# Transposing instructions in place of products with the identity, and a passage between two blocks without a phase barrier

## The chip, the cores and the metric

The kernel runs on one core of a Trainium2 chip. The metric is the device time of one execution in microseconds. A core has five engines with instruction streams of their own: PE (TensorE, matrix products into eight PSUM banks), DVE (VectorE), ACT (ScalarE), POOL (GpSimd) and SP (SyncE, which here issues the weight transfers). They meet through semaphores only.

## What is computed

Two blocks run one after the other on 256 tokens of width 1024, all in float32. The first: a token mixer, then 16 experts that each choose 34 of 272 tokens, then a norm. The second: a mixer with two branches (a gated delta rule and RWKV-7), whose context part does not depend on the first block, then a mixture of 32 experts in four groups. Cut to what the change touches:

```python
# end of block 1
y = einsum(hid, w_down) * g[..., None]           # 16 experts, scattered and added to h
h = h + y
x = _rmsnorm(h, final_norm_g)                    # over all 1024 columns, times a row of gains
# start of block 2
u = modulate(rmsnorm(x, norm_mix_g_2), shift, scale)
cols = u @ w_in_2                                # the mixer's projections
```

So two norms follow each other: the final norm of block 1 gives `x`, and the norm ahead of mixer 2 needs the sum of squares of `x`, that is of the normed rows times the gains.

## The kernel before

The kernel is one hand-written program; each engine's stream is written out in its own function, and the order in the code is the order on the engine. SP's queue carries almost all transfers, in order of issue. Weights pass through a ring of 6 slots: piece `n` may be issued once piece `n-6` has been used (`issue`, semaphore `piece_used`).

**Experts of block 1.** For each expert PE multiplies the gathered tokens `xsT` with eight gate and eight up pieces (`gate_up_pe`, L3026), turns the hidden rows with transposing instructions (`turn_hid_pe`, L3036) and multiplies with eight down pieces (`down_pe`, L3049). The context part of block 2 is threaded through this stage as a coroutine on each engine (`context_pe`, `context_dve`, `context_act`); there its helper `heads` (L2749) makes 128x128 products, some of them with the identity matrix `ident`, which turn a tile.

**The passage.** At the end the last pair of experts is added to the rows (`combine_pe`, L3056, into four banks; `add_rows_dve`, L1730, four adds). Then all engines meet at a barrier (`phase_ended`). SP loads the row of gains `g_rows` (L870) behind this barrier. ACT squares and sums each of the two row tiles and takes the roots (`norm_act`, L280 and L283), DVE takes reciprocals and scales (`norm_dve`, L290 and L292), DVE multiplies with the gains (L566), and the same norm runs once more for mixer 2: ACT L280 and L283, DVE L290 and L292 into `cn`. PE turns `cn` with 16 transposing instructions (`transposed_norm_pe`, L274) into eight banks, DVE applies modulation, one bank after the other, into `u2x_lat` (L2046), and after a second barrier PE starts the first projection of mixer 2 (`by_feature`, L303, two groups of 32 products each).

**Later.** In the gated delta rule beta is spread over rows by products with the identity (L3176), each between three other products of its head (L3174, L3177, L3178); DVE waits for these sixteen products of a direction (L2125). `row_of_columns_pe` (L3430) turns 32 columns, each spread over 128, by 32 products of 128x128 with the identity; ACT copies each eight of them out as a row (`row_act`, L1412) and takes a root in between (L1418), which waits for DVE's sum (L2342). In the mixture of experts each pair of experts runs: 32 products with gate and up (L3506), gathers (L3488), four products with the 64x64 identity that turn the hidden rows (L3515), gathers, eight products with down (L3529). Ten slots hold the weights there; SP issues a piece when its slot has been used.

`nc.tensor.transpose` and a product with the identity give the same tile: data as the loaded operand, identity streamed. The first is the engine's transposing form. In the trace a float32 product leaves two records, as L303 does with 64 products and 128 records, and a transposing instruction leaves one (L274: 16 and 16).

## Time and profile before

| | us |
|---|---|
| median of 3 runs | 2850.74 (2850.65 to 2860.58) |
| profiled execution | 2856.64 |
| its span | 2854.8 |
| PE busy | 2476.3 (87%) |
| DVE busy | 926.6 (32%) |
| ACT busy | 449.8 (16%) |

The span runs from the first to the last instruction of the profiled execution, and 1.84 us of its time lie outside. A busy share is an average over stages with different limits; the rows further below are of single stages. In a row, L3026 is line 3026 of the kernel before; `128*34 128x462` is a product with a loaded operand of 128 rows and 34 columns and a streamed one of 128 rows and 462 columns.

### The profile page before, as it was taken

The page shows a single profiled execution, that of the slowest core. Times are in us where ns is not written, and L with a number is a line of the kernel's source. Part 1 is how long each engine was busy: PE and PEld are TensorE (multiplying, and loading weights), DVE is VectorE, ACT ScalarE, POOL GpSimd, SP SyncE. Part 2 cuts the span into 40 slices and gives each one's busy share as a digit, 9 for nine tenths or more (in the row PEclk, how much of TensorE's full clock was granted, in tenths as well). Part 3 has the DMA queues.
Part 4 walks back from the last instruction along what each step waited for, and adds up shares of the span by engine and source line. Part 5 has one row for each costly group of instructions (what it writes and reads, how often), then busy time and mean ns, then how long its engine had stood idle before and what let it go on. Part 6 is the DMA issues. An engine that isn't in the chain of part 4 may idle for free. (4 is left out here: it accounts for less than half of the span.)

```text
span 2854.8 us, 43435 instructions
## 1 busy us (share of the span) xinstructions
PE 2476.3 (87%) x19563; PEld 1351.4 (47%) x19563; DVE 926.6 (32%) x1788; ACT 449.8 (16%) x810; POOL 85.1 (3%) x93
## 2 busy tenths in 40 slices
PE   6978588988999988999999999877686889689995
PEld 4524234333343333534444444355665888355553
DVE  1216733410423212241313141147547440332222
ACT  1022100110101010121211221022023220000001
POOL 0001000000000000000000000000000100000000
PEclk9987787999999999999999999978888999799998
DMA  5314433799999998999999999941010024359996
GB/s 183 118 59 157 168 138 152 316 411 393 419 406 415 417 417 370 380 417 416 411 416 406 415 398 418 413 157 60 2 38 1 3 94 148 144 235 422 422 422 282
DMA packets 129425, 789.13 MB, mean 276 GB/s; under 512 B 17473, under 2 KB 19785, under 8 KB 65113
## 3 DMA queue, kind: packets, MB, share of 16 engines
q1 hardware_dynamic: 125785, 773.78, 67.3%
q0 software_dynamic: 3456, 12.58, 1.1%
q8 instruction: 154, 2.52, 0.4%
q14 instruction: 30, 0.25, 0.0%
HBM read 774.79 MB, written 11.53 MB: 275 GB/s over the span
## 5 line engine op out<-in xcount | busy, mean ns | idle before, releaser
L3026 PE MATMUL bank<-ring,arena 128*34 128x462 f32 (+1 forms) x3072 | 673.5, 574 | 76.9 <-DMA ring<-in_w_up 58.2
L3026 PEld LDWEIGHTS bank<-ring,arena 128*34 128x34 f32 x3072 | 179.8, 113 | 434.9 <-issue 408.2
L3049 PE MATMUL bank<-ring,arena 128*34 128x512 f32 (+1 forms) x1536 | 340.2, 559 | 1.1 <-DVE arena L2032 0.6
L3049 PEld LDWEIGHTS bank<-ring,arena 128*34 128x34 f32 x1536 | 105.3, 112 | 217.0 <-issue 193.7
L303 PE MATMUL bank<-arena,ring 128*128 128x256 f32 (+1 forms) x688 | 161.1, 397 | 3.9 <-DVEq L2049 1.8
L303 PEld LDWEIGHTS bank<-arena,ring 128*128 128x128 f32 x688 | 135.7, 198 | 30.5 <-DVEq L2049 2.2
L2025 DVE TENSOR_TENSOR arena<-arena,bank 34x462 f32<-34x462 f32 (+1 forms) x96 | 95.3, 1081 | 154.1 <-ACT arena L1097 153.8
L1097 ACT ACTIVATE arena<-bank 34x462 f32<-34x462 f32 (+1 forms) x96 | 85.8, 1038 | 195.9 <-PE bank L3026 195.8
L3506 PE MATMUL bank<-ring,arena 128*64 128x256 f32 x992 | 111.1, 379 | 3.0 <-DMA ring<-in_moe_w_up 2.2
L313 PE MATMUL bank<-ring,arena 128*128 128x512 f32 (+1 forms) x224 | 98.8, 596 | 0.0
L2924 PEld LDWEIGHTS bank<-arena 64*64 64x64 f32 x2304 | 72.8, 134 | 48.3 <-issue 47.8
L3506 PEld LDWEIGHTS bank<-ring,arena 128*64 128x64 f32 x992 | 72.8, 137 | 45.1 <-issue 12.3
L3488 PE MATMUL bank<-arena 128*128 128x512 f32 (+1 forms) x160 | 82.6, 648 | 5.8 <-DVE arena L2505 5.8
L3422 PE MATMUL bank<-arena,ring 128*128 128x256 f32 x384 | 83.1, 379 | 0.0
L2924 PE MATMUL bank<-arena 64*64 64x64 f32 x2304 | 82.7, 221 | 0.0
L1981 DVE TENSOR_TENSOR arena<-arena,bank 128x256 f32<-128x256 f32 x40 | 15.0, 418 | 200.5 <-PE bank L2924 200.5
L3422 PEld LDWEIGHTS bank<-arena,ring 128*128 128x128 f32 x384 | 72.9, 190 | 9.9
L1132 ACT ACTIVATE arena<-bank 128x512 f32<-128x512 f32 x42 | 25.1, 597 | 318.8 <-PE bank L2924 212.7
L3529 PE MATMUL bank<-ring,arena 128*64 128x512 f32 x264 | 65.2, 624 | 2.7 <-issue 2.0
L2737 PE MATMUL bank<-arena,ring 128*128 128x256 f32 x288 | 64.2, 381 | 2.8 <-DMA ring<-in_w_in 2.8
L353 PE MATMUL bank<-ring,arena 128*128 128x512 f32 (+1 forms) x136 | 63.5, 622 | 3.6 <-DVE arena L2367 2.7
L954 POOL TENSOR_TENSOR arena<-arena 128x256 f32<-128x256 f32 (+1 forms) x16 | 26.6, 1662 | 1285.1 <-ACT arena L1221 1284.4
(634 smaller groups left out, 2904.1 us busy)
## 6 DMA issues: line engine op xcount, KB each, us to landing
ring<-in_w_gate SPq DMA_DIRECT2D x128, 1408.0 KB, 12.8
ring<-in_w_up SPq DMA_DIRECT2D x128, 1408.0 KB, 12.5
ring<-in_w_down SPq DMA_DIRECT2D x128, 1408.0 KB, 10.9
ring<-in_w_in SPq DMA_DIRECT2D x46, 1024.0 KB, 6.9
ring<-in_moe_w_down SPq DMA_DIRECT2D x33, 1024.0 KB, 15.3
ring<-in_moe_w_gate SPq DMA_DIRECT2D x31, 1024.0 KB, 13.3
ring<-in_moe_w_up SPq DMA_DIRECT2D x31, 1024.0 KB, 16.1
ring<-in_ada_w SPq DMA_DIRECT2D x24, 1024.0 KB, 7.0
```

The source lines that it names most:

```text
L303: last = mm(ps[base + ct][:, 0:n_toks], w[:, k, ct * P:(ct + 1) * P], x[:, half * kts + k, :], start=half + k == 0, stop=half == len(views ...
L313: last = mm(ps[base + t][:r, 0:w.shape[2]], x[:, half * kts + k, off:off + r], w[:, k, :], start=half + k == 0, stop=half == len(views) - ...
L1097: ACTV(hid_rows(c), in_rows(ps[c][0:CAP, 0:n]), ACT.Silu).then_inc(silu_done, up(silu_done))
L2025: TT(hid_rows(c), hid_rows(c), in_rows(ps[c][SLOT:SLOT + CAP, 0:n]), ALU.mult).then_inc(hid_done, up(hid_done))
L2737: last = mm(bank_a[:, ct % 2 * SEQ:(ct % 2 + 1) * SEQ], views[k // 4][0][:, k % 4, ct * P:(ct + 1) * P], u2x_ctx[:, k, :], start=k == 0, s ...
L2924: last = mm(dst[r, q, :], lhs[r, q, :], rhs[r, q, :], start=True, stop=True)
L3026: last = mm(ps[c][row:row + CAP, 0:n], xsT[:, e, k, :], w[:, at:at + n], start=k == 0, stop=k == KT - 1)
L3049: last = mm(ps[6][row:row + CAP, c:c + n], hidT[:, j, :], w[:, at - m * PIECE:at - m * PIECE + n], start=j == 0, stop=j == FT - 1)
L3422: last = mm(ps[base + ct // 2][:, ct % 2 * SEQ:(ct % 2 + 1) * SEQ], views[k // kts][0][:, k % kts, ct * P:(ct + 1) * P], x[:, k, :], start ...
L3488: last = mm(ps[gather_bank(g, k)][:, 0:group_cols(g)], xn2_by8[:, t, k, :], oh[g % 2][:, t, 0:group_cols(g)], start=t == 0, stop=t == 1)
L3506: last = mm(ps[4][CAP2 * which:CAP2 * (which + 1), m * DE:(m + 1) * DE], x, weights[which][:, k, :], start=k == 0, stop=k == KT - 1)
L3529: last = mm(ps[6 + half][CAP2 * m:CAP2 * (m + 1), :], hidT2[:, f, CAP2 * m:CAP2 * (m + 1)], w[:, f, half * BANK:(half + 1) * BANK], start= ...
```

## The change

Two things change. Products with the identity become transposing instructions: 48 in the context part (keys, values, beta of the delta rule, values of RWKV), 16 for beta (L3176), 32 in `row_of_columns_pe` and 78 in the mixture of experts. Other products with the identity stay.

The passage is rewritten. The first barrier is gone; PE, ACT and DVE go on by semaphores. DVE multiplies the un-normed rows with the gains at once (`scaled`), ACT sums the squares of the rows and of `scaled`, and the factor of the second norm is worked out from both sums on columns, so that one scaling with two factors gives `cn`. The rows `x1` themselves are scaled at the end, behind the modulation. PE turns `cn` tile by tile, and the first products of mixer 2 wait for four of the eight parts of `u2x_lat` (`ready`), not for a barrier. ACT asks for a root early, on a column that nobody reads, so that the table of roots is loaded then. SP loads `g_rows` ahead of the first piece of the seventh expert, and the first six pieces of mixer 2 right behind the last piece of the experts.

```diff
-        def by_feature(pe, base, views, x, n_toks):
+        def by_feature(pe, base, views, x, n_toks, ready=None):
             for half, (w, slot, count, _) in enumerate(views):
                 pe.wait_ge(slot, count)
+                if ready:
+                    pe.wait_ge(ready, due(pe, ready, w.shape[1]))
...
+        squares = xsT_flat[:, 2 * D:4 * D].rearrange("p (t d) -> p t d", t=2)
+        scaled = u2[:, 0:2, :]
+        scaled_sum, scaled_std, rstd_sq = st4[:, 0:2], st4[:, 2:4], den2[:, 0:2]
...
@@ SP
-            issue(tables_at, n_experts)
-            sp.wait_ge(phase_ended, N_PHASES_1 * 4)
+            gain_at = gate_up_pieces[6][0][0][3]
+            issue(tables_at, gain_at)
+            sp.wait_ge(piece_used, after(gate_up_pieces[3][KT - 1]))
             sp.dma_start(g_rows, A["final_norm_g"].partition_broadcast(P)).then_inc(g_rows_landed, up(g_rows_landed, 16))
+            issue(gain_at, n_experts)
+            issue(n_gdn - 8, n_gdn - 2)
             sp.wait_ge(final_ready, due(sp, final_ready))
             sp.dma_start(flat7, consts[2]).then_inc(join7_landed, up(join7_landed, 16))
-            issue(n_gdn - 8, n_gdn - 2)
@@ ACT
-            act.drain().then_inc(phase_ended, 1)
-            act.wait_ge(phase_ended, phase_end(act))
-            final_norm_act(act, x1)
-            act.wait_ge(final_ready, due(act, final_ready))
-            norm_act(act, x1, TILES2, cn)
+            ACTV(ss[:, 2:3], eps_col, ACT.Sqrt)
+            for t in range(2):
+                act.wait_ge(x_ready, due(act, x_ready))
+                ACTV(squares[:, t, :], x1[:, t, :], ACT.Square, accum_out=ss[:, t:t + 1]).then_inc(act_order, up(act_order))
+            act.wait_ge(act_order, own(act, act_order))
+            ACTV(ss[:, 0:2], ss[:, 0:2], ACT.Sqrt, scale=1.0 / D, bias=eps_col).then_inc(norm_std_ready, up(norm_std_ready))
+            for t in range(2):
+                act.wait_ge(x_ready, due(act, x_ready))
+                ACTV(squares[:, t, :], scaled[:, t, :], ACT.Square, accum_out=scaled_sum[:, t:t + 1]).then_inc(act_order, up(act_order))
+            act.wait_ge(act_order, own(act, act_order))
+            act.wait_ge(sqrt_asked, due(act, sqrt_asked))
+            for t in range(2):
+                ACTV(scaled_std[:, t:t + 1], scaled_sum[:, t:t + 1], ACT.Sqrt,
+                     scale=rstd_sq[:, t:t + 1], bias=eps_col).then_inc(norm_std_ready, up(norm_std_ready))
@@ DVE
-                signal = x_ready if (t, half) == HALVES[-1] else dve_order
+                signal = x_ready if half else dve_order
                 add_rows_dve(t, half, 2 * t + half, signal)
             dve.wait_ge(x_ready, own(dve, x_ready))
-            dve.drain().then_inc(phase_ended, 1)
-            dve.wait_ge(phase_ended, phase_end(dve))
             dve.wait_ge(g_rows_landed, due(dve, g_rows_landed, 16))
-            final_norm_dve(dve, x1, x1)
+            for t in range(2):
+                TT(scaled[:, t, :], x1[:, t, :], g_rows, ALU.mult).then_inc(x_ready, up(x_ready))
-            norm_dve(dve, x1, TILES2, cn)
+            dve.wait_ge(norm_std_ready, due(dve, norm_std_ready))
+            nc.vector.reciprocal(rstd[:, 0:2], ss[:, 0:2]).then_inc(dve_order, up(dve_order))
+            dve.wait_ge(dve_order, own(dve, dve_order))
+            STT(rstd_sq, rstd[:, 0:2], 1.0 / D, rstd[:, 0:2], ALU.mult, ALU.mult).then_inc(sqrt_asked, up(sqrt_asked))
+            dve.wait_ge(x_ready, own(dve, x_ready))
+            for t in range(2):
+                dve.wait_ge(norm_std_ready, due(dve, norm_std_ready))
+                nc.vector.reciprocal(scaled_std[:, t:t + 1], scaled_std[:, t:t + 1]).then_inc(dve_order, up(dve_order))
+                dve.wait_ge(dve_order, own(dve, dve_order))
+                TS(cn[:, t, :], scaled[:, t, :], rstd[:, t:t + 1], scaled_std[:, t:t + 1], ALU.mult, ALU.mult).then_inc(xn_ready, up(xn_ready))
             for k in range(KT):
                 dve.wait_ge(xnT_ready, due(dve, xnT_ready))
                 TS(u2x_lat[:, k, :], ps[k][:, 0:SEQ], gains[:, k, 0:1], mods[:, k, 0:1],
                      ALU.mult, ALU.add).then_inc(u2x_ready, up(u2x_ready))
-                dve.wait_ge(u2x_ready, own(dve, u2x_ready))
+            for t in range(2):
+                last = TS(x1[:, t, :], scaled[:, t, :], rstd[:, t:t + 1], None, ALU.mult)
+            last.then_inc(final_ready, up(final_ready))
@@ PE
+            for t in range(2):
+                pe.wait_ge(xn_ready, due(pe, xn_ready))
+                for k in range(KT):
+                    last = nc.tensor.transpose(ps[k][:, t * P:(t + 1) * P], cn[:, t, k * P:(k + 1) * P], ident)
+                    if t == 1:
+                        last.then_inc(xnT_ready, up(xnT_ready))
             pe.drain().then_inc(phase_ended, 1)
-            pe.wait_ge(phase_ended, phase_end(pe))
-            pe.wait_ge(xn_ready, due(pe, xn_ready))
-            transposed_norm_pe(pe, TILES2, cn)
-            pe.drain().then_inc(phase_ended, 1)
-            pe.wait_ge(phase_ended, phase_end(pe))
+            phase_end(pe)
-            by_feature(pe, 0, gdn_pieces[0], u2x_lat, SEQ)
+            by_feature(pe, 0, gdn_pieces[0], u2x_lat, SEQ, u2x_ready)
@@ row_of_columns_pe (L3430); in the same way the other places
-                    last = mm(ps[base + k // 4][:, k % 4 * P:(k % 4 + 1) * P], column(k).to_broadcast([P, P]), ident,
-                              start=True, stop=True)
+                    last = nc.tensor.transpose(ps[base + k // 4][:, k % 4 * P:(k % 4 + 1) * P], column(k).to_broadcast([P, P]), ident)
```

On DVE the passage reads as follows before, from the last adds to the modulation; what a row waits for stands in brackets, and several instructions of one kind in a row are counted (x2).

```order
L1730 TENSOR_TENSOR arena<-arena,bank 128x512 [waits banks_filled] x4
L290 RECIPROCAL small<-small 128x1 [waits x_ready,norm_std_ready,g_rows_landed,phase_ended]
L292 TENSOR_SCALAR arena<-arena,small 128x1024 [waits dve_order]
L290 RECIPROCAL small<-small 128x1 [waits norm_std_ready,dve_order]
L292 TENSOR_SCALAR arena<-arena,small 128x1024 [waits dve_order]
L566 TENSOR_TENSOR arena<-arena 128x1024 [waits xn_ready]
L566 TENSOR_TENSOR arena<-arena 128x1024 [waits dve_order]
L290 RECIPROCAL small<-small 128x1 [waits norm_std_ready,final_ready]
L292 TENSOR_SCALAR arena<-arena,small 128x1024 [waits dve_order]
L290 RECIPROCAL small<-small 128x1 [waits norm_std_ready,dve_order]
L292 TENSOR_SCALAR arena<-arena,small 128x1024 [waits dve_order]
L2046 TENSOR_SCALAR arena<-bank,arena 128x256 [waits xnT_ready,xn_ready]
```

After the change the same stretch of DVE's stream is this.

```order
L1736 TENSOR_TENSOR arena<-arena,bank 128x512 [waits banks_filled] x4
L2046 TENSOR_TENSOR arena<-arena 128x1024 [waits g_rows_landed,x_ready]
L2046 TENSOR_TENSOR arena<-arena 128x1024
L2049 RECIPROCAL small<-small 128x2 [waits norm_std_ready]
L2051 SCALAR_TENSOR_TENSOR small<-small 128x2 [waits dve_order]
L2055 RECIPROCAL small<-small 128x1 [waits norm_std_ready,x_ready]
L2057 TENSOR_SCALAR arena<-arena,small 128x1024 [waits dve_order]
L2055 RECIPROCAL small<-small 128x1 [waits norm_std_ready]
L2057 TENSOR_SCALAR arena<-arena,small 128x1024 [waits dve_order]
L2060 TENSOR_SCALAR arena<-bank,arena 128x256 [waits xnT_ready] x8
L2063 TENSOR_SCALAR arena<-arena,small 128x1024 x2
```

The multiplication with the gains (1024 columns, two of them) moved ahead of both norms, one long scaling per tile is left between the sums and the modulation, and the scaling of `x1` (the last row) moved behind the modulation.

On PE the passage before runs from the last adds into banks to the first products of mixer 2.

```order
L3056 MATMUL bank<-arena 128x512 [waits y_read,banks_read]
L3056 MATMUL bank<-arena 128x512 x3
L274 MATMUL bank<-consts,arena 128x128 [waits xn_ready,phase_ended]
L274 MATMUL bank<-consts,arena 128x128 x15
L303 MATMUL bank<-arena,ring 128x256 [waits slot0_landed,phase_ended]
L303 MATMUL bank<-arena,ring 128x256 x15
L303 MATMUL bank<-arena,ring 128x256 [waits slot1_landed]
```

After the change PE's stream is this.

```order
L3078 MATMUL bank<-arena 128x512 [waits y_read,banks_read]
L3078 MATMUL bank<-arena 128x512 x3
L3137 MATMUL bank<-consts,arena 128x128 [waits xn_ready]
L3137 MATMUL bank<-consts,arena 128x128 x7
L3137 MATMUL bank<-consts,arena 128x128 [waits xn_ready]
L3137 MATMUL bank<-consts,arena 128x128 x7
L305 MATMUL bank<-arena,ring 128x256 [waits u2x_ready,slot0_landed]
L305 MATMUL bank<-arena,ring 128x256 x15
L305 MATMUL bank<-arena,ring 128x256 [waits u2x_ready,slot1_landed]
```

The waits for `phase_ended` are gone, the turning waits once for each tile, and the products wait for `u2x_ready` in two halves.

SP's queue before, from the last pieces of the experts to the constants of the mixer (`in_final_norm_g` is the row of gains, `const` a table for the delta rule):

```order
L852 DMA ring<-in_w_up 128x2816 [waits piece_used]
L852 DMA ring<-in_w_down 128x2816 [waits piece_used] x9
L870 DMA arena<-in_final_norm_g 128x1024 [waits phase_ended]
L872 DMA arena<-const 128x1088 [waits final_ready]
L852 DMA ring<-in_w_in 128x4x512 [waits piece_used] x6
L878 DMA arena<-in_gdn_a_log 128x8 [waits phase_ended]
```

After the change, first the place of the gains in the middle of the experts, then the end of the experts:

```order
L849 DMA ring<-in_w_up 128x2816 [waits piece_used]
L849 DMA ring<-in_w_down 128x2816 [waits piece_used]
L868 DMA arena<-in_final_norm_g 128x1024 [waits piece_used]
L849 DMA ring<-in_w_gate 128x2816 [waits piece_used]
L849 DMA ring<-in_w_up 128x2816 [waits piece_used]
...
L849 DMA ring<-in_w_down 128x2816 [waits piece_used] x9
L849 DMA ring<-in_w_in 128x4x512 [waits piece_used] x6
L872 DMA arena<-const 128x1088 [waits final_ready]
L877 DMA arena<-in_gdn_a_log 128x8 [waits phase_ended]
```

The gains moved from behind the experts to a place among the pieces of the seventh expert, and the six pieces of `in_w_in` moved ahead of the wait for `final_ready`.

## Rows read from the trace of the kernel before

**Rows 1.** Busy time of the engines by stretch; at the end clock, DMA share, GB/s.

```profile
1180.00:1850.00 670.00, 638.25 (x5749) 277.33 (x5750) 170.23 (x327) 126.42 (x255) 26.60 (x16) 0.99 1.00 413
...
1878.00:1893.00 15.00, 9.21 (x29) 7.76 (x30) 6.44 (x16) 2.01 (x6) 0.00 (x0) 0.50 1.03 373
1894.00:1918.00 24.00, 24.00 (x113) 21.12 (x112) 10.04 (x22) 3.55 (x6) 0.00 (x0) 1.00 0.52 161
2336.00:2344.00 8.00, 7.75 (x66) 7.57 (x67) 7.34 (x8) 5.16 (x10) 0.00 (x0) 1.00 0.90 333
2478.00:2490.00 12.00, 10.66 (x48) 10.18 (x48) 3.81 (x11) 0.00 (x0) 0.00 (x0) 0.50 1.01 427
...
2600.00:2742.00 142.00, 142.00 (x876) 81.87 (x874) 38.33 (x62) 10.69 (x18) 4.80 (x9) 1.00 1.01 422
```

**Rows 2.** Timeline of PE between the blocks: start, us; in brackets the idle time before.

```profile
1864.04 3.67 PE L3056 MATMUL bank<-arena 128*128 128x512 f32 x8 [1.38 <-ACT arena L1106]
1881.97 3.65 PE L274 MATMUL bank<-consts,arena 128*128 128x128 f32 x16 [14.26 <-DVE arena L292]
1887.44 30.95 PE L303 MATMUL bank<-arena,ring 128*128 128x256 f32 x128 [1.82 <-DVEq L2049]
```

**Rows 3.** Timeline of DVE between the blocks.

```profile
1867.74 0.69 DVE L1730 TENSOR_TENSOR arena<-arena,bank 128x512 f32<-128x512 f32 x1 [0.17 <-PE bank L3056]
...
1873.76 0.75 DVE L292 TENSOR_SCALAR arena<-arena,small 128x1024 f32<-128x1024 f32 x1
1874.55 2.48 DVE L566 TENSOR_TENSOR arena<-arena 128x1024 f32<-128x1024 f32 x2
1879.88 0.16 DVE L290 RECIPROCAL small<-small 128x1 f32<-128x1 f32 x1 [2.85 <-ACT small L283]
...
1882.74 4.60 DVE L2046 TENSOR_SCALAR arena<-bank,arena 128x256 f32<-128x256 f32 x8 [0.92 <-PE bank L274]
```

**Rows 4.** Timeline of ACT between the blocks.

```profile
1868.51 1.06 ACT L280 ACTIVATE arena<-arena 128x1024 f32<-128x1024 f32 x1 [4.62 <-DVEq L2038]
...
1870.86 1.28 ACT L283 ACT_TABLE_LOAD   x1
1872.15 0.62 ACT L283 ACTIVATE small<-small 128x1 f32<-128x1 f32 x2
```

**Rows 5.** Timeline of the DMA issues of SP between the blocks.

```profile
1877.43 8.09 SPq L852 DMA_DIRECT2D ring<-in_w_in  x6
```

**Rows 6.** DMA issues, 1860 to 1876 us: KB, us from issue to landing.

```profile
arena<-in_final_norm_g SPq DMA_DIRECT2D x1, 512.0 KB, 3.8
```

**Rows 7.** Line 3149, transposing: records, length in ns (least, median, most), first and last start.

```profile
L3149 PE MATMUL bank<-consts,arena x16: 272/273/307, 1956.1 to 1958.6; 128*128 128x128 f32 x16
```

**Rows 8.** Timeline of PE: eight transposing instructions of line 3149.

```profile
1956.13 1.04 PE L3149 MATMUL bank<-consts,arena 128*128 128x128 f32 x8
```

**Rows 9.** Timeline of PE: eleven transposing instructions of 34 rows.

```profile
1838.84 0.87 PE L3036 MATMUL bank<-consts,arena 34*128 34x34 f32 x11
```

**Rows 10.** Line 3430, products with the identity: records, lengths in ns, first and last start.

```profile
L3430 PE MATMUL bank<-consts,arena x64: 275/275/347, 2336.1 to 2343.2; 128*128 128x128 f32 x64
```

**Rows 11.** Timeline of DVE where it waits for the products around line 3176.

```profile
1970.96 0.69 DVE L2125 TENSOR_TENSOR arena<-bank,arena 128x512 f32<-128x512 f32 x1 [5.66 <-PE bank L3178]
...
1974.51 0.69 DVE L2125 TENSOR_TENSOR arena<-bank,arena 128x512 f32<-128x512 f32 x1 [2.39 <-PE bank L3178]
```

**Rows 12.** Timeline of DVE beside `row_of_columns_pe`.

```profile
2339.80 1.22 DVE L2342 TENSOR_REDUCE arena<-arena 128x16 f32<-128x1024 f32 x1
```

**Rows 13.** Timeline of ACT beside `row_of_columns_pe`.

```profile
2341.00 1.28 ACT L1418 ACT_TABLE_LOAD   x1
```

**Rows 14.** Chain that ended last, mixture of experts: start, us, what.

```profile
2595.95 1.08 PE bank L3515 x8
...
2798.47 22.89 DMA ring<-in_moe_w_up
...
2826.10 0.70 PE bank L3515 x4
```

More of the change, by code:

```diff
@@ L557, in filled_with_pair @@
             return KT + PAIRS + 2 * (2 * i + EARLY + 1)
-        def final_norm_act(act, src):
-            norm_act(act, src, TILES2, u2)
-        def final_norm_dve(dve, src, dst):
-            norm_dve(dve, src, TILES2, u2)
-            for t in range(2):
-                signal = final_ready if t else dve_order
-                TT(dst[:, t, :], u2[:, t, :], g_rows, ALU.mult).then_inc(signal, up(signal))
-                dve.wait_ge(signal, own(dve, signal))
-        g_rows = xsT.rearrange("p e k s -> p (e k s)")[:, 0:D]
+        xsT_flat = xsT.rearrange("p e k s -> p (e k s)")
+        g_rows = xsT_flat[:, 0:D]
+        squares = xsT_flat[:, 2 * D:4 * D].rearrange("p (t d) -> p t d", t=2)
+        scaled = u2[:, 0:2, :]
+        scaled_sum, scaled_std, rstd_sq = st4[:, 0:2], st4[:, 2:4], den2[:, 0:2]
         final_ready, g_rows_landed = sem("final_ready"), sem("g_rows_landed")
         x1 = h1[:, 1:3, :]
-        N_PHASES_1 = 7
+        N_PHASES_1 = 6
         phases_before_second = N_PHASES_1
@@ L956, in _ @@
                         pool.wait_ge(steps7_ready, own(pool, steps7_ready))
-            pool.drain().then_inc(phase_ended, 1)
-            pool.wait_ge(phase_ended, phase_end(pool))
             pool.drain().then_inc(phase_ended, 1)
@@ L2744, in project, with turned_heads @@
                             copied_by_act(token)
+                def turned_heads(dst, src):
+                    for h in range(4):
+                        last = nc.tensor.transpose(dst[:, h * P:(h + 1) * P], src(h), ident)
+                    return last
                 def heads(dst, lhs, rhs):
@@ L2788, in context_pe @@
                     pe.wait_ge(turned_read, due(pe, turned_read))
-                    heads(bank_a, lambda h: kT_c[:, h, c * P:(c + 1) * P], lambda h: ident).then_inc(turned, up(turned))
+                    turned_heads(bank_a, lambda h: kT_c[:, h, c * P:(c + 1) * P]).then_inc(turned, up(turned))
                 yield from until(slot_number(1, 2))
@@ L2906, in context_pe @@
                     for q in range(4):
-                        last = mm(bank_a[0:C7, q * P:(q + 1) * P], vT7c[:, q, c * C7:(c + 1) * C7], ident, start=True, stop=True)
+                        last = nc.tensor.transpose(bank_a[0:C7, q * P:(q + 1) * P], vT7c[:, q, c * C7:(c + 1) * C7], ident)
                     token = for_dve(last)
@@ L3175, in _ @@
                            start=True, stop=True)
-                        mm(ps[b0 + 1][:, hs], beta[:, c, e:e + 1].to_broadcast([P, P]), ident, start=True, stop=True)
+                        nc.tensor.transpose(ps[b0 + 1][:, hs], beta[:, c, e:e + 1].to_broadcast([P, P]), ident)
                         last = mm(ps[b0 + 2][:, hs], kT[:, h, toks], kT[:, h, toks], start=True, stop=True)
@@ L3514, in _ @@
                     for m, tau in enumerate(tiles_of(i)):
-                        last = mm(ps[4][:, f * P + m * CAP2:f * P + (m + 1) * CAP2], hid2_by2[0:CAP2, m, f, :],
-                                  ident[0:CAP2, 0:CAP2], start=True, stop=True)
+                        last = nc.tensor.transpose(ps[4][:, f * P + m * CAP2:f * P + (m + 1) * CAP2], hid2_by2[0:CAP2, m, f, :],
+                                                   ident[0:CAP2, 0:CAP2])
                 last.then_inc(hidT_ready, up(hidT_ready))
```

4 lines of the change are left out of this document (2 added, 2 removed).

## The prediction

> **What bounds the kernel now.** I read the stages first, by the busy time of the engines in stretches, because the 87% of PE are an average. In the second half of the experts of block 1 the transfers run at a DMA share of 1.00 and 413 GB/s while PE is busy 638 of 670 us; in the mixture of experts, 2600 to 2742 us, the DMA share is 1.01 at 422 GB/s and PE is busy all of the 142 us [rows 1]. In both stages PE and the transfers are close to each other, and the reader should see that taking work from PE there need not bring time. Between these stages the DMA is mostly free and a chain of PE, DVE and ACT sets the time.
>
> The passage is such a chain. The timelines show PE finish its last adds, stand idle 14.26 us, turn 16 tiles, and idle 1.82 us more before the projection [rows 2]. From DVE's last add (1867.74 + 0.69 = 1868.43) to the first product of L303 (1887.44) pass 19.0 us [rows 2, 3]. Transfers aren't late in it: the row of gains takes 3.8 us [rows 6] beside ACT's first norm, and the products at 1887.44 were released by DVE [rows 2].
>
> **The passage after the change.** I lay out the new chain with the durations of before, allowing some 0.1 us for each handover.
> - ACT sums a tile in (1870.86 − 1868.51)/2 = 1.18 us and takes a root in 0.31; the table load of 1.28 moves into ACT's idle time ahead of the last add [rows 4]. The first tile's sum fits ahead of the last add too. The second tile: 1868.5 to 1869.7, both roots in one instruction to 1870.0.
> - Beside it DVE multiplies with the gains, 2.48 us [rows 3], to 1871.0, and then makes two small columns of some 0.16 each [rows 3] by 1871.4. This multiplication was on the chain; now it is beside ACT's sum for its first half.
> - ACT sums the scaled tiles from 1870.0 to 1872.4; the first root is there at 1872.7.
> - DVE: reciprocal 0.16 and scaling 0.75 [rows 3], first tile at 1873.75, second at 1874.75. The scaling has two factors now. No row has that over 1024 columns in SBUF; below it costs 0.75, above 1.3 us (the multiplication's 1.24 rounded up). I take 0.75, since it is the same instruction and size as L292.
> - PE turns the first tile from 1873.9. L274 took 3.65 us for 16 at the granted clock 0.50 (1.2 GHz) [rows 1, 2], and an instruction has 0.42 of drain, so 0.215 each: the first bank is complete at 1873.9 + 8 × 0.215 + 0.42 = 1876.0.
> - DVE modulates in 4.60/8 = 0.575 us a bank [rows 3]; four banks, 1878.4. PE may start at 1878.5.
>
> So PE starts 1887.4 − 1878.5 = **8.9 us** earlier; 8.0 if the scalings cost their upper bound, 9.8 if PE turns at 2.4 GHz, where one costs 0.11 (below). What was put behind costs nothing: scaling `x1` (two of 0.75) ends near 1882.3, and ACT and DVE are next wanted when PE has finished 32 products of the first group, which alone took about half of 30.95 us [rows 2]. SP's six pieces of `in_w_in`, issued from 1877.43 before [rows 5], go out as slots come free and land while PE idles. Every stage behind follows this chain, and later transfers are issued off it, so the gain should reach the end.
>
> **The gains' transfer** moves into the saturated experts. 512 KB at 413 GB/s are **1.3 us** of a queue that ends the stage [rows 1, 6]. Bounds: nothing, if PE is the later one just there; 3.8 us, its whole time from issue to landing when alone [rows 6].
>
> **Transposing instructions.** The identity products leave two records each: L3430 has 64 for 32 products, first start to last (2343.2 − 2336.1)/63 = 0.113 us a record [rows 10], so 0.225 a product. Eight transposing ones take 1.04 us with a last one of 0.27 [rows 7, 8], so (1.04 − 0.27)/7 = 0.11 each. A turned 128x128 tile thus saves 0.115 us. The Trainium skill's page "TensorE: Matmul & The Clock Gate", section "Terms", calls the transposing mode four times faster for float32. The rows say twice, and they decide; by the page a product would save 0.17 and the beta term below would be 2.7 instead of 1.8.
> - Beta (L3176), 16 products: DVE waits 5.66 and 2.39 us for exactly these groups [rows 11], so 16 × 0.115 = **1.8 us** are on the chain. Bounds 0.9 (one direction hidden) and 3.6 (all at 1.2 GHz, at twice the price).
> - `row_of_columns_pe`, 32 products: PE saves 3.7 us. But ACT's root waits for DVE's sum, which ends at 2339.80 + 1.22 = 2341.0 [rows 12] and doesn't move. ACT's copies ended just there, and then the table load of 1.28 stood in front of the root, from 2341.0 to 2342.3 [rows 13]. With copies done early the load is over when the sum comes: **1.1 us**, bounds 0 (the load waits as well) and 3.7.
> - Mixture of experts, 78 products: eight records cost 1.08 us a pair [rows 14]. A turned tile of 64 columns lies between 0.065 (34 columns: (0.87 − 0.22)/10, a last one estimated from the 0.27 of the wide ones [rows 7, 9]) and 0.11, say 0.08, so a pair saves 0.75. Over 19.5 pairs that is 14.6 us on PE, but the chain ends in a transfer that waits 22.89 us behind others [rows 14] at 422 GB/s. Only the first pair (it releases slots before the queue is full) and the last four records of 0.70 behind the last transfer count: 0.75 + 0.35 = **1.1 us**.
> - Context part, 48 products: 5.5 us of PE under transfers with share 1.00 [rows 1]. Some fall early, where the ring isn't yet full; I take **0.9**, bounds 0 and 5.5.
>
> **Sum:** 8.9 + 1.8 + 1.1 + 1.1 + 0.9 − 1.3 = 12.5 us. The profiled execution took 2856.64 us (span 2854.8 and 1.84 around it), 5.9 above the median of the runs; I expect about 2844.1 for a like execution and **2850.74 − 12.5 = 2838.2 us** for the median. A measurement here tells about 0.5% (14.3 us) from no change, so this lies just inside.
>
> **Rivals.**
> - *PE, not the transfers, ends the mixture of experts.* For it: PE is busy 142 of 142 us [rows 1]. Against it: the DMA share of 1.01 and the 22.89 us [rows 1, 14]. Then 13.5 us come on top: 26 us, 2825. Chance 0.08.
> - *The clock falls behind the transposing rows.* Now 7.4 us of products keep 2.4 GHz, clock 1.00 [rows 1]; L274's turning ran at 0.50 throughout [rows 1, 2]. If the merge starts at 1.2 GHz and takes as long to recover as L303 did (clock 0.50 up to at least 1893, that is 5.6 us of its own work [rows 1, 2]), half of that is lost, about 3 us, and the 1.1 with it: gain 8.4, 2842. Chance 0.14. The same page of the Trainium skill, section "Part 4: PE-mode transpose", says that the full clock doesn't engage in transposing mode; by that rule this rival is what happens. The trace bears it out only so far that L274 stayed at 0.50, and there PE had idled before; no run here shows a long row of transposing that begins at the full clock.
> - *A new wait takes a third of the passage*, for instance ACT's second pair of sums behind DVE's multiplication, or scalings of 1.3 us with slow handovers: gain about 9, 2842. Chance 0.10.
> - *Slower than before: the clock stays low behind the rows.* From 2478 to 2490 PE is busy 10.66 of 12 us and yet at 0.50 all the time [rows 1], so busy work doesn't always bring 2.4 GHz back. A us at 1.2 GHz on the chain costs half a us. From 25 us on the whole gain is spent; 40 us give 2838.2 + 20 = 2858; slower by 0.5% begins at 54 us. Against it: L303 in the passage was back at 1.00 from 1894 on [rows 1], some 6 us after its start. Chance 0.03.
>
> **How the numbers follow.** The forecast has the remaining 0.65, with 2832 to 2844 as its own range. The 0.8 range reaches from 2828 (context or the rows at their upper bounds, part of the mixture) to 2848 (the gains at 3.8, no gain at the rows, clock lost): about 0.1 is left out on either side. Over 0.5% faster, below 2836.5: about 0.24 of the forecast's 0.65 and the 0.08 of the mixture, 0.32. Slower by as much: 0.02 of the last rival's 0.03. The rest is 0.66.
>
> **What the profile after would show.** PE's idle time ahead of the turning near 6 us instead of 14.3, and its first projection some 10 us behind DVE's last add; no table load between the sums. Lines with transposing instructions have half the records of before, 0.11 us apart. In the mixture PE waits more for transfers while the DMA share stays at 1.01. The granted clock behind the rows stays 1.00. The prediction is wrong if PE waits for `in_w_in` at the projection, if DVE's scaling with two factors takes well over a us, if the experts of block 1 end more than 2 us later, or if the mixture of experts gets shorter by more than 3 us.

## The result, and the profile after

The changed kernel takes **2833.98 us** (median of 5 runs, 2828.31 to 2835.56); the kernel before, in the same session, 2851.0 (2850.65 to 2860.58). The ratio is 0.9919, with a 95% interval from 0.9900 to 0.9937. The median lies in the predicted range (2828 to 2848), but 4.2 us under the predicted 2838.2; by the ratio, 2850.74 × 0.9919 = 2827.6, the time lies just under the range. The gain is over the 0.5% below which I had put most of the chance. The profiled execution took 2835.56 us (span 2833.7), against 2856.64 for that of before: 21.1 us less where my sum says 12.5.

Stretches of the changed kernel, with the columns of [rows 1]: length, busy time of PE, weight loads, DVE, ACT and POOL, granted clock, DMA share, GB/s.

```profile
1180.00:1850.00 670.00, 636.53 (x5719) 270.73 (x5720) 168.74 (x324) 125.92 (x255) 26.74 (x16) 0.98 0.99 411
1870.10:1880.30 10.20, 8.68 (x28) 7.32 (x29) 7.01 (x18) 0.04 (x1) 0.00 (x0) 0.50 0.08 14
2319.00:2323.00 4.00, 3.68 (x32) 3.47 (x32) 3.88 (x5) 2.55 (x5) 0.00 (x0) 1.00 0.75 243
2446.90:2464.00 17.10, 3.62 (x16) 3.27 (x16) 11.81 (x19) 4.17 (x7) 0.00 (x0) 0.50 0.62 203
2464.00:2467.40 3.40, 2.79 (x26) 2.79 (x26) 0.49 (x2) 0.00 (x0) 0.00 (x0) 1.00 1.01 426
2467.40:2491.00 23.60, 9.64 (x26) 6.30 (x26) 12.06 (x60) 1.70 (x3) 0.00 (x0) 0.50 0.66 277
2580.00:2722.00 142.00, 139.84 (x858) 79.04 (x856) 39.12 (x64) 11.29 (x19) 5.28 (x10) 1.00 1.01 422
```

The experts and the mixture stand as before, at a DMA share of 0.99 and 1.01. Around the passage the half-speed stretch is 10.2 us long; before, it still held at 1893 [rows 1], and the clock records, the trace's list of when the granted clock changed, put it at 1869.8 to 1893.7. New is the row at 2464.00: 3.4 us at 1.00 in the middle of the routing, which before is one stretch at 0.50 (2467.1 to 2511.5 by the clock records; a part of it in [rows 1]).

PE's timeline in the passage, as in [rows 2]:

```profile
1861.45 3.67 PE L3078 MATMUL bank<-arena 128*128 128x512 f32 x8 [1.37 <-ACT arena L1103]
1871.03 3.68 PE L3137 MATMUL bank<-consts,arena 128*128 128x128 f32 x16 [5.91 <-DVE arena L2057]
1875.30 30.34 PE L305 MATMUL bank<-arena,ring 128*128 128x256 f32 x128 [0.59 <-DVE arena L2060]
```

From the last combine to the first product of the projection pass 10.77 us instead of 20.33 (differences of the first starts of the last instruction of one line and the first of the other). PE's idle time is 5.91 and 0.59 where it was 14.26 and 1.82 [rows 2]. DVE's and ACT's timelines, as in [rows 3, 4, 12, 13]:

```profile
1865.16 0.69 DVE L1736 TENSOR_TENSOR arena<-arena,bank 128x512 f32<-128x512 f32 x1 [0.17 <-PE bank L3078]
1865.88 2.36 DVE L2046 TENSOR_TENSOR arena<-arena 128x1024 f32<-128x1024 f32 x2
...
1869.96 0.16 DVE L2055 RECIPROCAL small<-small 128x1 f32<-128x1 f32 x1 [1.44 <-ACT small L1261]
1870.16 0.81 DVE L2057 TENSOR_SCALAR arena<-arena,small 128x1024 f32<-128x1024 f32 x1
...
1873.25 3.71 DVE L2060 TENSOR_SCALAR arena<-bank,arena 128x256 f32<-128x256 f32 x8 [1.36 <-PE bank L3137]
...
2323.02 1.22 DVE L2358 TENSOR_REDUCE arena<-arena 128x16 f32<-128x1024 f32 x1
```

```profile
1861.33 1.28 ACT L1249 ACT_TABLE_LOAD   x1
...
1867.07 0.30 ACT L1254 ACTIVATE small<-small 128x2 f32<-128x2 f32 x1
...
1868.31 1.04 ACT L1257 ACTIVATE arena<-arena 128x1024 f32<-128x1024 f32 x1
...
1869.47 0.66 ACT L1261 ACTIVATE small<-small 128x1 f32<-128x1 f32 x2
...
2322.52 1.28 ACT L1424 ACT_TABLE_LOAD   x1
2324.28 0.31 ACT L1424 ACTIVATE arena<-arena,small 128x16 f32<-128x16 f32 x1 [0.48 <-DVE arena L2358]
```

DVE's last add ends at 1865.85, ACT's last root at 1869.47 + 0.66, DVE scales at 1870.16 and PE turns at 1871.03: each link is within some 0.6 us of where the prediction put it, counted from the last add, with the table load before the add and the gains' multiplication beside the sums. The last two ACT rows are those of `row_of_columns_pe`: the copies are done at 2322.5, the load (1.28) is over at 2323.8, and the root at 2324.28 waits for DVE's sum that ends at 2324.24. Before, the load began when the sum came [rows 12, 13].

Two lines with transposing instructions, as in [rows 10]: records, lengths in ns (least, median, most), first and last start.

```profile
L3452 PE MATMUL bank<-consts,arena x32: 272/273/295, 2319.3 to 2322.7; 128*128 128x128 f32 x32
...
L3536 PE MATMUL bank<-consts,arena x78: 277/280/329, 2513.0 to 2805.7; 64*128 64x64 f32 x78
```

32 records instead of 64, and 78 instead of 156; the 32 stand (2322.7 − 2319.3)/31 = 0.11 us apart, at 1.00. The chain that ended last still runs through transfers in the mixture, as in [rows 14]:

```profile
2720.21 21.19 DMA ring<-in_moe_w_up
...
2777.98 22.81 DMA ring<-in_moe_w_up
```

### The profile page after: what moved, and what is told of

Same layout as the page of the kernel before. It is cut to its first block and busy times, and to the rows that moved or that the text cites. A ratio compares the mean times of both kernels' runs of the same rounds, so it can differ in the third digit from the quotient of the medians.

```text
span 2833.7 us, 43073 instructions
## 1 busy us (share of the span) xinstructions
PE 2455.0 (87%) x19389; PEld 1321.6 (47%) x19389; DVE 924.3 (33%) x1788; ACT 449.1 (16%) x810; POOL 85.1 (3%) x93
## 6 DMA issues: line engine op xcount, KB each, us to landing
ring<-in_w_down SPq DMA_DIRECT2D x128, 1408.0 KB, 10.8
```

## Experiments

Each kernel has a trace. The table gives what passes between first starts of PE's lines in it, in us: from the experts' first product to the last combine, from there to the projection's first product, from there to the first group of gated delta products, from there to the rows' first instruction (gated delta and RWKV), from the rows to the merge, from the last merge product to the mixture's loop, and from there to the last product. The merge itself takes 82.8 us in every trace and has no column. "Turnings" are transposing instructions, "products" are products with the identity. Two kernels, before and changed, were traced twice.

| kernel | experts | passage | projection | gated + RWKV | rows | routing | mixture |
|---|---|---|---|---|---|---|---|
| before | 1411.0 | 20.3 | 78.0 | 370.6 | 11.5 | 93.0 | 307.2 |
| before again | 1407.5 | 20.3 | 74.7 | 370.6 | 11.5 | 93.0 | 309.1 |
| context only | 1400.8 | 20.3 | 74.7 | 370.7 | 11.5 | 93.0 | 309.2 |
| rows only | 1409.8 | 20.3 | 72.2 | 375.7 | 10.3 | 90.8 | 309.8 |
| beta only | 1407.8 | 20.3 | 77.9 | 370.5 | 11.5 | 93.1 | 307.0 |
| all turnings, old passage | 1404.2 | 20.3 | 77.9 | 370.6 | 10.3 | 90.8 | 306.6 |
| passage only | 1412.1 | 10.8 | 72.2 | 375.9 | 11.5 | 93.1 | 309.1 |
| changed | 1408.1 | 10.8 | 74.7 | 369.3 | 10.3 | 90.8 | 306.6 |
| changed again | 1408.5 | 10.8 | 74.5 | 369.2 | 10.3 | 90.8 | 309.1 |
| changed, mixture by products | 1410.8 | 10.8 | 72.2 | 369.0 | 10.3 | 90.8 | 309.1 |
| changed, rows by products | 1407.8 | 10.8 | 72.2 | 368.9 | 11.5 | 93.0 | 306.8 |
| changed, gains late | 1407.6 | 10.8 | 72.2 | 368.8 | 10.3 | 90.8 | 306.4 |
| changed, context by products | 1408.6 | 10.8 | 74.6 | 369.4 | 10.3 | 90.8 | 306.2 |
| the same, gains late | 1411.7 | 10.8 | 74.6 | 369.2 | 10.3 | 90.8 | 309.8 |
| changed, PE busy in the passage | 1407.6 | 9.8 | 74.9 | 370.7 | 10.3 | 90.8 | 306.8 |
| changed, PE busy in the routing | 1408.4 | 10.8 | 74.5 | 369.1 | 10.3 | 89.4 | 307.6 |
| gains late, PE busy in the routing | 1404.2 | 10.8 | 72.2 | 368.9 | 10.3 | 85.2 | 308.7 |

How to read it: the passage, the rows and the routing repeat to 0.1 us and are worth arguing about to that depth. The experts differ by 3.5 us and the mixture by 2 between two executions of one kernel, and the projection takes one of three lengths, 72.2, some 74.7 or 78.0.

### The parts by themselves

`x1`: before with all turnings. `x2`: changed with all of them back to products. `x3`: before with the context's turnings alone. `x4`: changed with the mixture's back to products.

```diff
# x1 (and x3 for the context part alone), e.g.
- mm(ps[b0 + 1][:, hs], beta[:, c, e:e + 1].to_broadcast([P, P]), ident, start=True, stop=True)
+ nc.tensor.transpose(ps[b0 + 1][:, hs], beta[:, c, e:e + 1].to_broadcast([P, P]), ident)
# x2: the same lines of the changed kernel the other way; x4: line 3536 alone
```

> The kernel before with all transposing instructions and the old passage. By the terms of my sum it gains 1.8 + 1.1 + 1.1 + 0.9 = 4.9 us, 2846. Theory 'the context part pays more than its term, since nothing delays the experts here': the experts of block 1 end 3 to 5 us earlier, and with beta 1.25, the rows 1.2 and the mixture 0.6 the gain is 6 to 8 us, 2843 to 2845. Rival 'the passage alone gives the gain': no change beyond 2 us, 2849 to 2851. The projection behind the passage should lie as far ahead of before's as the experts' end does, no more.

Ratio 0.9957 (0.9944 to 0.9970), median 2845.6 against 2855.97: some 12 us by the ratio and 10.4 by the medians, more than the theory's 6 to 8. The experts are 3 to 7 us shorter than in the two executions of before, the routing 2.2, the rows 1.2; the projection as long as in the longest case of before. The rival falls.

> The changed kernel with all transposing instructions turned back into identity products: the new passage alone. By the terms of my sum it gains 8.9 - 1.3 = 7.6 us, 2843.4. Theory 'the half-speed stretch of the projection gets shorter by the passage itself': the first product lies 9.6 us earlier against the last combine and the first group of gated delta products 13 us earlier, total gain 10 to 12 us, 2839 to 2841. Rival 'the clock's stretches are chance of one execution': the projection stage is as long as before, gain 8 to 9 us. Rival 'the gains' transfer costs its whole 3.8': the experts end 3 to 4 us later than before, gain 5 us.

Ratio 0.9972 (0.9961 to 0.9983), 2848.73: some 8 us, at the sum's 7.6. PE's timeline:

```profile
1865.54 3.67 PE L3072 MATMUL bank<-arena 128*128 128x512 f32 x8 [1.38 <-ACT arena L1103]
1875.11 3.49 PE L3131 MATMUL bank<-consts,arena 128*128 128x128 f32 x16 [5.90 <-DVE arena L2057]
1879.38 27.86 PE L305 MATMUL bank<-arena,ring 128*128 128x256 f32 x128 [0.78 <-DVE arena L2060]
```

The passage is again 10.8 us. The projection is 72.2 us, 2.5 to 5.8 less than in both executions of before, so the first group of gated delta products lies 12.0 to 15.3 us earlier against the last combine, as the theory has it. But the gated delta and RWKV stages then take 5.2 us more, as they do in the other kernel with a projection of 72.2 and beta by products (the rows alone, below): by the clock records 114.4 us of them run at half speed, against 98.9 in both executions of before. So the total fits the sum of my terms, and the "10 to 12" of the theory isn't borne out. The rival with the whole 3.8 is not excluded: the experts are 1.1 to 4.6 us longer than in the two of before, and the interval of the ratio goes from 4.9 to 11.1 us.

> The kernel before with the context part's 48 transposing instructions alone. By the term of my sum 0.9 us gained, 2850. Theory 'the context part pays nearly its whole 5.5 us on PE': the experts end 4 to 5 us earlier and the time falls as much, to 2846. Rival 'the transfers set the end of the experts, what PE gains is taken back by the last expert': PE is some 5 us ahead at expert 6 and less than 1 us at the last combine, 2850.

Ratio 0.9993 (0.9981 to 1.0006), medians 2852.23 against 2855.97. Its trace has the experts at 1400.8, 6.7 to 10.2 us under the two of before; but that execution, at 2845.68, was the shortest of twelve. By the ratio the part is worth between nothing and some 5 us, which decides neither for the theory nor for the rival.

> The changed kernel with the 78 turnings of the mixture of experts made identity products again. Theory 'transfers end the mixture': 0.6 to 1.1 us longer than the changed kernel, 2835. Rival 'PE ends it': 78 x 0.18 = about 14 us longer, 2848. The DMA share from 2580 to 2720 should stay at 1.0 in both.

Ratio 0.9939 (0.9920 to 0.9958), 2837.28. A stretch of the mixture in it:

```profile
2580.00:2722.00 142.00, 142.00 (x886) 82.56 (x884) 39.65 (x64) 11.29 (x19) 4.97 (x10) 1.00 1.01 422
```

PE is busy all 142 us with products, 139.84 with turnings (above), and the DMA share is 1.01 in both. The mixture takes 306.2 to 309.8 us with turnings and 307.0 to 309.8 with products; 306.6 and 309.1 with turnings, 307.2 and 309.1 with products, in two executions each of changed and before. "PE ends it", 14 us, is refuted. The ratio is 0.0020 (5.7 us) over the changed kernel's, more than the 0.6 to 1.1 expected, but the two intervals overlap.

### Repeats, the gains' place, and a busy PE

> The changed kernel once more, beside the next three. Theory 'the clock's stretches follow the lengths of PE's waits': the half-speed stretch around the passage is again about 10 us long (7 to 11, not the 20 to 24 of the old passage), and the routing has again a short stretch at 1.00 near its middle; time 2830 to 2836. Rival 'chance of one execution': a stretch of 20 us in the passage, or the routing 2.4 us longer.

2834.82 (ratio 0.9918, 0.9902 to 0.9933). The half-speed stretch around the passage lies at 1870.3 to 1880.5, the projection is 74.5 and the routing 90.8 long: all as in the first execution. Over all traces the stretch around the old passage lasts 13.7 to 23.9 us by the clock records, and around the new one 3.4 to 10.2 (leaving out the kernel where PE is busy there): shorter with the new passage every time, but not of one length.

> The changed kernel with the row of gains loaded behind the last piece of the experts' weights. By the term of my sum 1.3 us faster than the changed kernel. Theory 'it eats most of what the context part gained': the last combine lies 3 to 6 us earlier, 2829. Rival 'PE is the later one there and the transfer is hidden': no change. If the row comes too late for the passage, ACT or DVE waits at the multiplication with the gains, by at most 3.8 us less what PE's last products cover.

```diff
- issue(tables_at, gain_at)
+ issue(tables_at, n_experts)
  ...
  sp.dma_start(g_rows, A["final_norm_g"].partition_broadcast(P)).then_inc(g_rows_landed, up(g_rows_landed, 16))
- issue(gain_at, n_experts)
```

2830.18 (0.9900, 0.9882 to 0.9918), 4.6 us under the run beside it, with overlapping intervals. In the changed kernel the row's transfer, issued at 946.31 among expert 6's pieces, takes this long from issue to landing (KB, us):

```profile
arena<-in_final_norm_g SPq DMA_DIRECT2D x1, 512.0 KB, 11.3
```

When alone it was 3.8 [rows 6]. Issued behind the last piece (SP's timeline):

```profile
1845.94 0.43 SPq L867 DMA_DIRECT2D arena<-in_final_norm_g  x1
```

it has landed when the passage wants it: the passage stays at 10.8. The experts' 1407.6 says nothing by itself; the last combine lies 0.7 and 1.2 us earlier than in the two traces of the changed kernel, not 3 to 6.

> The changed kernel with 23 more products of ones that nobody reads, between the last combine and the turning, so that PE isn't idle there. Theory 'what PE does in the wait sets the clock behind it': the granted clock stays 1.00 in the turning and the projection, the 16 turnings take 1.9 instead of 3.7 us, and the first group of gated delta products lies 3 to 5 us earlier against the last combine; 2830. Rival 'the clock falls anyway there, as it does at other places in busy work': no change, or 1 us slower if the last filler ends behind the scaled tile.

```diff
+ for n in range(23):
+     mm(ps[7][:, 0:P], C["ones"], C["ones"], start=True, stop=True)
  for t in range(2):
      pe.wait_ge(xn_ready, due(pe, xn_ready))
```

2835.94 (0.9918, 0.9901 to 0.9936): no gain. PE's timeline and two stretches:

```profile
1863.74 5.30 PE L3135 MATMUL bank<-consts 128*128 128x128 f32 x46
1869.81 2.01 PE L3139 MATMUL bank<-consts,arena 128*128 128x128 f32 x16 [0.77 <-DVE arena L2057]
1873.14 27.86 PE L305 MATMUL bank<-arena,ring 128*128 128x256 f32 x128 [1.32 <-DVE arena L2060]
```

```profile
1860.20:1903.70 43.50, 41.38 (x225) 35.73 (x225) 24.29 (x51) 12.78 (x24) 0.00 (x0) 1.00 0.54 179
1903.70:1910.50 6.80, 6.80 (x17) 4.38 (x17) 6.31 (x14) 2.44 (x3) 0.00 (x0) 0.50 0.17 63
```

The clock did stay at 1.00 in the turning, and the 16 turnings took 2.01 us instead of 3.68. But the projection then waits 1.32 us for DVE, and a half-speed stretch of 6.8 us comes while PE is busy all the time, at 1903.7. From the last combine to the rows 112.6 us run at half speed by the clock records, against 109.2 and 109.3 in the two executions of the changed kernel: what the passage won (0.94), the later stages gave back. The theory is right for the turning and wrong for the projection and on the worth.

> The changed kernel with 46, 30 and 20 such products in PE's three waits of the routing stage (15.6, 8.2 and 5.8 us). Theory as above: the clock stays at 1.00 through the routing, the start of the mixture's loop lies 4 to 6 us earlier against the last merge product, and as the mixture's end is set by transfers that are issued from there, at least half of it reaches the end: 2830. Rival 'the half-speed stretches there don't follow PE's idle time': no change or up to 2 us slower. If the mixture's end doesn't move with its start, the transfers of its first tiles were ahead of PE.

The same two lines, with 46, 30 and 20, ahead of the waits for `half_ready`, `mask_ready` and `onehot_ready`. 2832.05 (0.9911, 0.9895 to 0.9927); the first lot ended 2.2 us late for the turnings, so the stage got only 1.4 us shorter, not 4 to 6.

### Both together, before once more, and a table of two by two

> The changed kernel with the row of gains behind the experts' pieces and with 32, 30 and 18 products that nobody reads in the three waits of the routing (46, 30 and 20 in the last try, where the first lot ended some 2 us too late). If the two gains add up: 4 from the gains' place and 4 to 5 from the routing, of which the last transfers take back about 1, so 2826 to 2828. If the gains' place was chance of six runs: 2830 to 2832. The turnings of the routing should start no later than in the changed kernel against the last merge product.

**2827.16 us** (0.9896, 0.9878 to 0.9914), the lowest median here, some 7 us under the changed kernel's; the intervals of the ratios overlap, so that the whole gain is indicated and the shorter routing alone is shown. PE's timeline and stretches of its routing:

```profile
2443.95 8.80 PE L3485 MATMUL bank<-consts 128*128 128x128 f32 x64 [6.01 <-DVEq L2394]
2453.42 1.97 PE L3489 MATMUL bank<-consts,arena 128*128 128x128 f32 x16 [0.67 <-DVE arena L2403]
2456.78 3.73 PE L3495 MATMUL bank<-arena 128*128 128x36 f32 x32 [1.40 <-DVE arena L2406]
...
2475.78 14.13 PE L3513 MATMUL bank<-arena 128*128 128x512 f32 x32 [1.66 <-DVE arena L2519]
```

```profile
2440.10:2446.90 6.80, 2.95 (x14) 2.95 (x15) 3.58 (x6) 2.92 (x5) 0.00 (x0) 0.50 0.21 22
2446.90:2460.50 13.60, 11.53 (x101) 11.13 (x101) 8.00 (x14) 1.25 (x3) 0.00 (x0) 1.00 0.95 360
2460.50:2464.00 3.50, 3.50 (x19) 3.50 (x19) 1.46 (x9) 1.49 (x2) 0.00 (x0) 0.51 1.00 419
2464.00:2490.00 26.00, 24.25 (x122) 19.88 (x121) 14.81 (x59) 0.21 (x1) 0.00 (x0) 1.00 0.46 191
```

PE is at 1.00 for most of it: 13.7 us of the stage run at half speed, against 44.4 in the changed kernel, and it is 5.6 us shorter.

> The kernel before once more, for a second trace of it. Theory 'the length of PE's wait in the passage sets the half-speed stretch there': again 20 to 24 us at 1.2 GHz around it, and one long stretch in the routing with no 1.00 inside. Rival 'chance': 10 us or less. How far its last combine lies from the first trace's (1867) tells how much of the differences in the experts is chance: by the spread of its times I expect up to 5 us.

2849.89 us. Stretches at half speed:

```profile
1864.80:1885.20 20.40, 6.50 (x23) 5.59 (x24) 10.73 (x22) 5.70 (x11) 0.00 (x0) 0.50 0.68 246
2458.70:2503.00 44.30, 18.69 (x65) 14.96 (x66) 22.06 (x76) 5.87 (x10) 0.00 (x0) 0.50 0.67 259
```

20.4 us around the passage and one stretch in the routing, as expected (the 13.7 us above are of another kernel with the old passage, the rows alone); yet its projection was 74.7, not 78.0, and its last combine came 5.1 us earlier. So 3.3 us of the projection, and as much or more in the experts, is chance of an execution.

> The changed kernel with the context part's 48 turnings made identity products again, the gains where the change puts them. By my term (0.9) it is 0.9 us longer than the changed kernel. Theory 'the context part pays 4 to 5 us in the experts': 4 to 5 us longer, 2838 to 2840.

> The same with the row of gains behind the experts' pieces. With the three others it makes a table of two by two. Theory 'the gains' transfer costs where PE has won time, and is hidden where PE is the later one': no difference to the run with the gains in their place, while with turnings the late gains give 1 to 4 us. Rival 'it is a fixed price of the DMA': the same 1 to 4 us faster here too.

Medians, with the gains in place and late: 2834.82 and 2830.18 with the context's turnings, 2836.48 (0.9922, 0.9909 to 0.9934) and 2835.72 (0.9920, 0.9907 to 0.9932) with products. The turnings are worth 1.7 us with the row in place and 5.5 with it late; the late row 4.6 and 0.8. That is the pattern of the last theory, though the context part is worth 1.7 here and not the 4 to 5 of the theory before it. The intervals of all four ratios overlap. The experts' column of the table points the same way: with the context's turnings they take 1404.2 us in the mean without the row among their pieces (four traces, 1400.8 to 1407.6) and 1408.5 with it (six, 1407.6 to 1410.8); with products 1409.6 without (five) and 1410.4 with it (two). So the turnings are worth 5.4 and 1.9 there, and the row costs 4.3 and 0.8. With 3.5 us between two executions of one kernel it is indicated, not shown.

### Where the routing's 2.2 us come from

> The kernel before with the 32 turnings of the row of columns alone. Theory 'the rows' 1.2 us shift the work against the clock's half-speed stretches': from the rows' first instruction to the first merge product 1.24 us less, and from the last merge product to the mixture's loop 2.2 us less, with a stretch at 1.00 inside the routing. Rival 'the beta turnings, or chance, do that': the routing as long as before, 93.0 us from the last merge product.

> The kernel before with the 16 beta turnings alone. By my term the gated delta part from its first products to the turning of its output is 1.8 us shorter; the traces so far say 1.25 in the first group. The routing as long as before by the theory of the rows; 2.2 us shorter by the rival.

> The changed kernel with the row of columns made of identity products again. Theory: the first merge product comes 1.24 us later, and the routing is 2.2 us longer than in the changed kernel, one stretch at 0.50 without a gap. Rival: 1.24 us, and the routing as in the changed kernel.

One run each: 2854.82, 2852.41 and 2835.78 us, beside 2848.33 for before. Executions of before lie up to 17.8 us apart (2847.11 to 2864.88), so single times say nothing here; the traces do. Stretches of the routing with the rows alone turned, and of the changed kernel with the rows by products:

```profile
2462.40:2479.50 17.10, 3.65 (x16) 3.27 (x16) 11.81 (x19) 4.17 (x7) 0.00 (x0) 0.50 0.60 200
2479.50:2482.90 3.40, 2.82 (x26) 2.85 (x26) 0.43 (x2) 0.00 (x0) 0.00 (x0) 1.00 1.02 431
2482.90:2506.80 23.90, 9.94 (x26) 6.27 (x26) 12.07 (x60) 1.70 (x3) 0.00 (x0) 0.50 0.66 276
```

```profile
2447.20:2491.50 44.30, 18.71 (x65) 14.96 (x66) 22.03 (x76) 5.87 (x10) 0.00 (x0) 0.50 0.67 259
```

With the rows turned there is the 3.4 us at 1.00 and the routing takes 90.8; without, one stretch of 44.3 us at 0.50 and 93.0. It holds in all seventeen traces, apart from the two kernels that fill the routing. The rows' theory is shown. The beta turnings alone bring nothing to the end of their stages (370.5 against 370.6): the first group is 1.25 us shorter, and 0.86 of it is lost again in the next. In that trace 102.2 us of the two stages run at half speed, against 98.9 before.

## Why the prediction was wrong

**The sum, 12.5 us, was too small.** The step that failed is "Every stage behind follows this chain": the stages behind were taken to be as long as before, and the clock entered only as a rival that takes something away. It gave instead: 2.4 us between the projection and the rows, over what I had for beta, and 2.2 us in the routing.
- *The passage*: forecast 8.9, measured 9.56 in every trace with the new one (10.5 where PE was kept busy in it). Scaling with two factors cost 0.81 (I took 0.75), and the modulation 0.46 a bank instead of 0.575, with the wait behind each instruction gone. No new wait took a share of it. Right.
- *Behind the passage*: no term. The projection took 78.0 and 74.7 in the two executions of before, and 72.2 to 74.7 in all nine of the changed kernel and its variants with beta turned (without the one where PE was kept busy in the passage). From the projection's first product to the rows the four kernels with old passage and beta products take 445.3 to 448.6 us, mean 446.8; the two with beta turned and the old passage 448.4 and 448.5; the new passage alone 448.1; both together 441.0 to 444.0 in nine traces, mean 442.6. So 4.2 us come out where I had 1.8 for beta, and neither edit brings any of it alone. The time at half speed goes with it. The projection takes 72.2 us in the six traces with less than 2 us of it at half speed, 74.5 to 74.9 in the eight with 6.2 to 10.2, and 77.9 or 78.0 in the three with some 16.5; three of them, before, changed and gains late, with the mean granted clock at 0.89, 0.96 and 0.99:

```profile
1887.40:1965.40 78.00, 71.45 (x288) 54.37 (x288) 51.47 (x88) 23.26 (x36) 0.00 (x0) 0.89 0.45 146
1875.30:1950.00 74.70, 67.75 (x289) 51.91 (x289) 54.36 (x94) 23.37 (x36) 0.00 (x0) 0.96 0.37 115
1874.60:1946.80 72.20, 65.25 (x289) 50.11 (x289) 54.30 (x94) 23.37 (x36) 0.00 (x0) 0.99 0.38 118
```

From the projection to the rows 112.2 us run at half speed in the mean of the four, 101.7 in that of the nine, and 116.0 to 118.8 with one of the two edits alone. What puts a stretch where it falls no run shows, and which of the lengths an execution gets can't be told ahead.

- *Beta*: the term of 1.8 was mis-sized as a term of its own: 1.25 in the first group, nothing by the end of the stages when alone, where 3.3 us more ran at half speed.
- *Rows*: 1.1 forecast, 1.24 measured, by the very load I named. The clock stayed at 1.00 behind them (to 2416.2 by the clock records), so the rival with the slower clock is refuted. The Trainium skill's page "TensorE: Matmul & The Clock Gate", section "Part 4: PE-mode transpose", says the full clock doesn't engage in transposing; the 32 records at 1.00 above don't agree. PE was at 1.00 when they began; whether turnings alone bring the clock up, no run here shows. What I had not foreseen is **2.2 us in the routing**, from the rows' 1.24 alone.
- *Mixture*: 1.1 forecast. The lower of the two lengths fell by 0.6, the upper not at all; means over eight traces with turnings and seven with products (without those that fill the routing) are 307.3 and 308.6, with executions 2 us apart. The 1.3 between them is mostly how often the lower length came (six of eight, two of seven), which may be chance. The mechanism, transfers at the end, is right.
- *Context and gains*: −0.9 and +1.3 forecast. The experts took 1407.5 to 1411.0 us in the four traces without either (before, before again, rows only, beta only; mean 1409.0) and 1407.6 to 1410.8 in the six with both in place (changed, again, mixture or rows by products, the two with a busy PE and the gains in place; mean 1408.5). The net is near nothing, as forecast, but that is luck: by the table of two by two and the experts' means the turnings bring some 5 us and the row takes some 4 back (indicated only), so both terms were too small and cancel.

By the traces that is 9.6 + 4.2 + 1.2 + 2.2 + 1.3 + 0.5 = 19.0 us, between the 17.0 of the medians and the 23 of the ratio (0.0081 × 2851; 18 to 28.5 by its interval). The 6.5 us over my sum are the projection's 2.4, the routing's 2.2, the passage's 0.7, and 1.2 in the three other terms. A second, smaller fault is the base: 2850.74 was the median of three runs, and later sessions gave 2855.97 (27 runs) and 2858.4 (11); the ratio doesn't suffer from that.

**Open:** what sets the experts' 3.5 us of spread, and where the half-speed stretches fall, and with them the projection's length. Only single executions have a trace.

## What to carry to other kernels

A chain between two stages can be forecast to half a us by laying out its links with the trace's own durations, and then the stages behind it must be asked what the earlier start does to the clock. Where two edits share a stage (a release on PE and a new transfer, here in the experts), cost them together: the one can eat the other. A filled wait keeps the granted clock up, but it pays only where the time at half speed doesn't come back in the work behind it: it fell from 44.4 to 13.7 us in the routing, and rose by 3.4 us from the passage to the rows.

## What the runs showed of the hardware

- A turning by the transposing instruction costs half of the product with the identity for float32: one record of 0.11 us instead of two. It runs at 1.00 as well: 32 of them in 3.68 us.
- A small shift can change where half-speed stretches fall. One of 1.24 us made one of 44.4 us in the routing into two, with 3.4 us at 1.00 between, and was worth 2.2 us there in every trace.
- PE kept busy through the wait of the passage had its half-speed stretch later, in the midst of full work (6.8 us at 1903.7).
- The same stage of the same kernel takes another length with another time at half speed: the projection of before 78.0 us with 16.5 at half speed, and 74.7 with 9.8.
